# Gate and up products of the FFNs as groups of two by two tiles with seven products

## The reference

```python
def swiglu(u, w_gate, w_up, w_down):              # D_FF = 2816
    return (jax.nn.silu(u @ w_gate) * (u @ w_up)) @ w_down
for l in range(DEPTH):                            # DEPTH = 2
    mod = c_act @ w_ada[l] + b_ada[l]
    sh1, sc1, g1, sh2, sc2, g2, sh3, sc3, g3 = jnp.split(mod, N_MOD, axis=-1)
    x = x + 0.5 * g1 * swiglu(modulate(x, sh1, sc1), ffn1_gate[l], ffn1_up[l], ffn1_down[l])
    x = x + g2 * token_mix(modulate(x, sh2, sc2), ...)
    x = x + 0.5 * g3 * swiglu(modulate(x, sh3, sc3), ffn2_gate[l], ffn2_up[l], ffn2_down[l])
# hybrid layer, at its end: D_FF_2 = 4096
x = x + jnp.square(jax.nn.relu(h2 @ w_up)) @ w_down
```

## Time and profile before

| | |
|---|---|
| median of 3 runs | 3493.08 us (3489.26 to 3496.66) |
| profiled execution | 3486.15 us, of which the span is 3484.4 us |
| TensorE busy | 3432.2 us (99%) |
| VectorE busy | 1755.6 us (50%) |
| ScalarE busy | 1182.7 us (34%) |
| GpSimd busy | 269.2 us (8%) |
| clock granted to TensorE, mean | 0.992 |

### The profile page before, as it was taken

The page is one execution under the profiler, slowest core; times in us unless marked ns, Lnnn a source line. Parts: engine busy times, 40 slices in busy tenths (PEclk is TensorE's granted clock), DMA queues, the critical chain, the costliest instruction groups (busy, mean ns, idle before and its releaser), DMA issues.

```text
span 3484.4 us, 40863 instructions
## 1 busy us (share of the span) xinstructions
PE 3432.2 (99%) x16696; PEld 2744.1 (79%) x16696; DVE 1755.6 (50%) x3034; ACT 1182.7 (34%) x1989; POOL 269.2 (8%) x226
## 2 busy tenths in 40 slices
PE   8999999999999999999999999999999999999999
PEld 7888786777888788887777878887778777878887
DVE  7666456565666733334654643334553555364433
ACT  3222236543222222223555332223322444223322
POOL 0000210002000200021100100013011000120000
PEclk9999999999999999999999999999999999999999
DMA  7565321123565533233210322322221223122332
GB/s 251 206 209 187 105 92 60 43 68 120 189 218 194 184 99 101 93 95 105 74 49 25 115 85 85 109 83 93 73 85 64 72 65 120 40 94 91 98 102 79
DMA packets 120361, 376.36 MB, mean 108 GB/s; under 512 B 13296, under 2 KB 28272, under 8 KB 120176
## 3 DMA queue, kind: packets, MB, share of 16 engines
q1 hardware_dynamic: 120176, 373.76, 32.7%
HBM read 371.61 MB, written 2.10 MB: 107 GB/s over the span
## 4 chain that ended last, share of the span: by engine, by line
PE 93%; DVE 4%; ACT 2%; issue 0%; POOL 0%; DMA 0%; SPq 0%; ACTq 0%; POOLq 0%; DVEq 0%
PE ps L449 26%; PE ps L451 26%; PE ps L450 26%; PE ps L670 2%; PE ps L693 2%; PE ps L565 2%; PE ps L492 1%; PE ps L483 1%; PE ps L484 1%; PE ps L485 1%; PE ps L499 1%; DVE s_wl L1459 1%; PE ps L504 0%; ACT s_wh L961 0%; PE ps L532 0%
## 5 line engine op out<-in xcount | busy, mean ns | idle before, releaser
L1459 DVE TENSOR_TENSOR s_wl<-s_raw,s_wh 128x1024 fp32r<-128x1024 f32 (+3 forms) x645 | 704.8, 1094 | 892.7 <-ACT s_wh L961 891.9
L449 PE MATMUL ps<-s_uh,s_wh 128*128 128x512 f32 x2824 | 1129.8, 400 | 17.0 <-ACT s_sg L1201 4.5
L451 PE MATMUL ps<-s_ul,s_wh 128*128 128x512 f32 x2824 | 1106.3, 392 | 0.0
L450 PE MATMUL ps<-s_uh,s_wl 128*128 128x512 f32 x2824 | 1105.5, 391 | 0.0
L961 ACT ACTIVATE s_wh<-s_raw 128x1024 fp32r<-128x1024 f32 (+3 forms) x645 | 588.0, 913 | 734.5 <-PE ps L451 543.1
L449 PEld LDWEIGHTS ps<-s_uh,s_wh 128*128 128x128 f32 x2824 | 533.7, 189 | 161.0 <-issue 43.2
L451 PEld LDWEIGHTS ps<-s_ul,s_wh 128*128 128x128 f32 x2824 | 533.3, 189 | 113.4
L450 PEld LDWEIGHTS ps<-s_uh,s_wl 128*128 128x128 f32 x2824 | 533.9, 189 | 108.2 <-issue 2.2
L451 PE MATMUL ps<-s_fl,s_wh 128*128 128x512 f32 x960 | 378.2, 394 | 0.0
L449 PE MATMUL ps<-s_fh,s_wh 128*128 128x512 f32 x960 | 378.2, 394 | 0.0
L450 PE MATMUL ps<-s_fh,s_wl 128*128 128x512 f32 x960 | 378.2, 394 | 0.0
(11 more groups left out here) (406 smaller groups left out, 3342.6 us busy)
## 6 DMA issues: line engine op xcount, KB each, us to landing
s_raw<-w SPq DMA_DIRECT2D x616, 512.0 KB, 3.6
s_raw<-w SPq DMA_DIRECT2D x96, 192.0 KB, 2.4
s_raw<-w SPq DMA_DIRECT2D x64, 256.0 KB, 2.6
s_raw<-w SPq DMA_DIRECT2D x19, 128.0 KB, 2.1
s_x<-x SPq DMA_DIRECT2D x4, 512.0 KB, 6.8
out<-s_x SPq DMA_DIRECT2D x8, 256.0 KB, 2.5
s_raw<-w SPq DMA_DIRECT2D x4, 420.0 KB, 4.3
s_crow<-crow SPq DMA_DIRECT2D x2, 512.0 KB, 6.0
```

The lines of the kernel that those rows point to most:

```text
L449: TE.matmul(o, w_hi(i, k), h, start=first, stop=False)
L450: TE.matmul(o, w_lo(i, k), h, start=False, stop=False)
L451: return TE.matmul(o, w_hi(i, k), l, start=False, stop=last)
L1459: V.tensor_tensor(wl[w][:, 0:n], raw[t % NRAW][:, 0:n], wh[w][:, 0:n].bitcast(F32), SUB).then_inc(*s_lo.up(("lo", t)))
```

## The change

Two column tiles (A, B of the output), two tiles of input features (k1, k2) and two halves of the tokens (256 each) are a product of two 2x2 block matrices. Instead of eight block products it makes seven, between sums of weight blocks and sums of activation blocks (the Winograd form of Strassen's scheme), and combines the results. This holds for gate and up from column tile 2 on (from 6 on in `f10`, from 4 on in `up`); the tiles before are as they were, and so are the down products.

- A weight tile is now two feature tiles by 256 columns (128x512, 256 KB); there are four for a group of gate or up. VectorE and GpSimd extend it in place to seven blocks (128x896): VectorE one sum, GpSimd three differences. ScalarE and VectorE split 896 columns into high part and rest.
- The activation side has four block combinations for each pair of feature tiles (`th`, `tl`), made once a stage: GpSimd four differences of 128x256 for each of four pairs, from an unsplit copy `uu` that ScalarE now also writes; ScalarE the high part, VectorE the rest, beside the first plain column tiles.
- TensorE runs 21 matmuls of 256 columns a weight tile, into four banks for a group.
- Combining: ScalarE copies the first product out of PSUM, VectorE adds the others in four operations (`combine`). SiLU, product, high part and rest then handle 1024 columns at once.
- Rounds are 12 and 10 column tiles (12, 10, 10 in `up`).
- Side tiles: one behind every fourth weight tile of a group, one more behind the second tile of up where jj < 14, and as before behind plain and down tiles. `f20` keeps 48 of its 72, `f11` gets 24.

```diff
+SEVEN = ((0, 3, 0), (2, 0, 0), (5, 0, 1), (4, 1, 0), (1, 1, 1), (6, 2, 0), (3, 2, 1))
+def side_at(x, j, kp):
+    return kp == 3 or kp == 1 and x == "u" and j < 14
 # tensor_engine
+        def seven(g, name, c, banks, st):
+            o = [take((g, q), b) for q, b in enumerate(banks)]
+            for kp in range(4):
+                i = get(name, 2 * kp, c * 128)
+                pe.wait_ge(*s_dve["t", st, kp])
...
+                for n, ((unit, q, half), (h, l)) in enumerate(zip(SEVEN, right)):
+                    out = o[q][:, 256 * half:256 * half + 256]
+                    w = slice(128 * unit, 128 * unit + 128)
+                    TE.matmul(out, wh[slot[i]][:, w], h, start=kp == 0 and half == 0, stop=False)
+                    TE.matmul(out, wl[slot[i]][:, w], h, start=False, stop=False)
+                    ins = TE.matmul(out, wh[slot[i]][:, w], l, start=False, stop=kp == 3 and (half == 1 or q == 3))
 # scalar_engine, get
-                    act.wait_ge(*landed(t))
+                    act.wait_ge(*(s_pool["weights", t] if todo[t][5] == "seven" else landed(t)))
 # vector_engine, get
+            while added[0] <= min(i + NRAW - 1, len(todo) - 1):
+                t = added[0]
+                added[0] += 1
+                if todo[t][5] == "seven":
+                    w = raw[t % NRAW]
+                    dve.wait_ge(*landed(t))
+                    V.tensor_tensor(w[:, 512:640], w[:, 128:256], w[:, 384:512], ADD).then_inc(*s_dve.up(("S1", t)))
...
-                    n, w = todo[t][2] * todo[t][4], slot[t]
+                    n, w = 896 if todo[t][5] == "seven" else todo[t][2] * todo[t][4], slot[t]
+            def combine(x_, jj, q):
...
+                V.tensor_tensor(q[:, 0:5:4, :], q[:, 3:4, :].broadcast_to([128, 2, 256]), two_(0), ADD)...
+                dve.wait_ge(*s_pe["ps", (g_, "all")])
+                dve.wait_ge(*s_dve.now())
+                V.tensor_tensor(q[:, 1:3, :], q[:, 4:5, :].broadcast_to([128, 2, 256]), two_(1), ADD)...
+                dve.wait_ge(*s_dve.now())
+                V.tensor_tensor(q[:, 3, :], q[:, 2, :], bank((g_, 1))[:, 0:256], ADD)...
+                dve.wait_ge(*s_dve.now())
+                V.tensor_tensor(q[:, 1:3, :], q[:, 1:3, :], two_(2), ADD)...
 # pool_engine
+        def weights(st):
+            for kp in range(4):
...
+                PO.tensor_tensor(q[:, 0, :], k1[:, 256:512], k1[:, 0:256], SUB)...
+                PO.tensor_tensor(q[:, 1, :], k2[:, 256:512], q[:, 0, :], SUB)...
+                PO.tensor_tensor(q[:, 2, :], q[:, 1, :], k1[:, 0:256], SUB)...
+                PO.tensor_tensor(q[:, 3, :], k2[:, 0:256], q[:, 1, :], SUB)...
...
+                    pool.wait_ge(*s_dve["S1", i])
+                    PO.tensor_tensor(w(5), w(4), w(0), SUB).then_inc(*s_pool.up(("S2", i)))
+                    PO.tensor_tensor(w(1), w(0), w(1), SUB).then_inc(*s_pool.up(("S3", i)))
+                    pool.wait_ge(*s_pool["S2", i])
+                    PO.tensor_tensor(w(6), w(2), w(5), SUB).then_inc(*s_pool.up(("S4", i), ("weights", i)))
```

More of the change, by code:

```diff
@@ L7, with rounds, single, mixed_at @@
 AHEAD = 2
-CHUNK_FF = 11
+ROUND = 12
 def chunks(n, step):
     return [(a, min(step, n - a)) for a in range(0, n, step)]
+def rounds(nf):
+    return [(0, ROUND)] + [(a, min(10, nf - a)) for a in range(ROUND, nf, 10)]
+def single(u, first):
+    return 6 if first else 2 if u else 4
+def side_at(x, j, kp):
+    return kp == 3 or kp == 1 and x == "u" and j < 14
+def mixed_at(u, first):
+    if first:
+        return {4: ((0,), (1,)), 5: ((2,), (3,))}
+    return {0: ((0, 1), ()), 1: ((2,), (3,))} if u else {0: ((0, 1), ()), 2: ((2,), ()), 3: ((3,), ())}
+SEVEN = ((0, 3, 0), (2, 0, 0), (5, 0, 1), (4, 1, 0), (1, 1, 1), (6, 2, 0), (3, 2, 1))
 def plan():
@@ L30, in ffn @@
     def ffn(g, u, d, nf, ahead=False):
-        for a, n in chunks(nf, CHUNK_FF):
+        for a, n in rounds(nf):
             for j in range(a, a + n):
@@ L34, in ffn @@
                     continue
-                if j == 0 and u:
+                if j >= single(u, ahead):
+                    for x, name in (("g", g), ("u", u)) if u and j % 2 == 0 else (("g", g),) if j % 2 == 0 else ():
+                        for kp in range(4):
+                            t.append((name, 2 * kp, 2, j * 128, 256, "seven"))
+                            if side and side_at(x, j, kp):
+                                t.append(side.pop(0))
+                elif j == 0 and u:
                     pair(g, 0, u, 0)
@@ L518, in ffn @@
             tiles.side = list(ADA.get(st, []))
+            at = ring[1]
+            halves = [[ring[0][(at + 4 + q) % 8] for q in range(4)], [ring[0][(at + q) % 8] for q in range(4)]]
+            assert len(ring[0]) == 8
             if first:
@@ L536, in ffn @@
                             ins.then_inc(*s_pe.up(*([("w", i)] if n == 7 else []), *([("ps", f)] if k == 7 else [])))
-            for a0, n in chunks(nf, CHUNK_FF):
+            for a0, n in rounds(nf):
                 for jj in range(a0, a0 + n):
@@ L540, in ffn @@
                         continue
-                    if jj == 0:
+                    if jj >= single(u, first):
+                        if jj % 2 == 0:
+                            p = 0 if u else jj // 2 % 2
+                            seven(("g", st, jj), g, jj, halves[p], st)
+                            if u:
+                                seven(("u", st, jj), u, jj, halves[1], st)
+                            ring[1] = at + (4 if u or p else 0)
+                    elif jj == 0:
                         fm_pair(("g", st, 0), g, 0, ("u", st, 0) if u else ("g", st, 1), u or g, 0 if u else 1, ("u", st))
@@ L1571, in ffn @@
                     low(fl[:, j, :], s[:], fh[:, j, :], s_act["hh", st, jj], ("h", st, jj))
-                for m in range(8):
-                    fm(d, n, m, a0, st)
+                begin = max(a0, plain)
+                for jj in range(begin, a0 + n, 2):
+                    for kp in range(4):
+                        get(g, 2 * kp, jj * 128)
+                        if side_at("g", jj, kp):
+                            side(st)
+                        if jj > begin and kp == 0 and not u:
+                            product(jj - 2)
+                        if jj > begin and kp == (0 if u else 1):
+                            hidden(jj - 2, a0)
+                    combine("g", jj, quad[0 if u else jj // 2 % 2])
+                    for kp in range(4 if u else 0):
+                        get(u, 2 * kp, jj * 128)
+                        if side_at("u", jj, kp):
+                            side(st)
+                    if u:
+                        combine("u", jj, quad[1])
+                        product(jj)
+                last = a0 + n - 2
+                for m in range(8):
+                    for k0, nk in chunks(n, 8):
+                        get(d, a0 + k0, m * 128)
+                        side(st)
+                        if m == 0 and k0 == 0:
+                            if not u:
+                                product(last)
+                            hidden(last, a0)
                     gate = mod[:, MOD[st] + 16 + m:MOD[st] + 17 + m] if st in MOD else None
```

153 lines of the change are left out of this document (135 added, 18 removed).

## The result

The changed kernel takes 3702.4 us (median of 4 runs, 3695.4 to 3703.9) against 3491.2 us for the kernel before on the same chip: a ratio of 1.061, 95% interval 1.059 to 1.062, slower by 211 us. The profiled execution of the changed kernel is 3703.9 us, with a span of 3702.1, that is 218 us above the profiled one of before; its mean granted clock is 0.969 for 0.992.

The account below looks back on a forecast made before the run. TensorE bounds the kernel before; after the change VectorE was to set the pace. Pairs +107, round ends +17 and stage starts +15 us make +139 on 3493: 3632 us, range 3490 to 3710.

Parts of the forecast that it names:

- rival (D): Whole kernel: each turn costs 0.31 us and hits all VectorE operations, landing takes 3.6, TensorE's clock falls: 3758 us; chance 0.08.
- TensorE's gain: Gate and up: 21 matmuls of 256 columns at 119.7 ns make a pair 20.1 us for 21.75, 75 us less.
- Rival (C): Matmuls of 256 columns don't come under 129.6 ns, weight load setting the pace: 3647 us; inside the forecast's 0.70.
- VectorE sets these paces: Gate and up: VectorE's work, port losses and transfer wait set the time of a pair; +107 us over all pairs.
- The wait for a transfer: Inside up, VectorE's sum waits some 2.4 us for the buffer a side tile frees, once per three-side pair.
- The paces: Gate and up, us a pair: three side tiles 27.4, two 24.3, none 20.8, last FFN 24.1; +107 us in all.
- The turns: VectorE operations with two SBUF sources lose 0.27 us each to a pending GpSimd difference; 13 losses, 3.5 us a pair.
- The last FFN: Two groups there have two products and rests: 19.8 us plus 4.3 of port losses, 24.1 a pair for 21.75.
- The clock: TensorE's clock, 1.00 in the FFN windows before, falls in places only in the worse case that totals 3758 us.
- Starts and ends: FFN stages: late hidden values at round ends +17 us, activation sums and first weight sums at starts +15 us.
- (A): Gate and up: port turns cost nothing, GpSimd fitting into the combinings and waits: 3501 us; chance 0.10.
- (B): Side tile operations and buffer wait also stay hidden, TensorE sets the pace in all pairs: 3428 us; chance 0.12.

Follow-up runs that it names:

- both suspects small: Changed kernel with side tile operations over 128 columns and GpSimd's differences over 16, results incomplete: 3518.5 us, 1.009 of the kernel before.

## Why the prediction was right, and where its sizes were not

The forecast was 3632 us, in a range from 3490 to 3710; 3702 is inside, 8 us from its end, and on the side that had 0.80. The increase was 211 us where 139 were forecast. That it lies inside is partly luck: the pairs with side tiles (30.4 and 26.8 us) lie nearer to rival (D), 31.5 and 26.4, than to the forecast's 27.4 and 24.3, and two errors the other way, VectorE's work and the last FFN, kept the total down. Of the signs that the prediction named, VectorE is at 76% and not over 90% with side tiles, the lo pass has a mean of 1.20 and not 1.3 us, TensorE without side tiles is idle 8% and not 3%. By its steps:

- **TensorE's gain** was right: 119.7 ns from start to start for 256 columns was forecast, and the trace of the changed kernel has 26 steps in the 3.02 us between these two lines, 116.2 ns. So the pair is 19.5 to 19.7 us where TensorE bounds it (forecast 20.1). Rival (C), a floor of 129.6 ns, fell.

```profile
1639.95 0.28 PE L525 MATMUL ps<-s_uh,s_wh 128*128 128x256 f32 x1
...
1642.97 0.28 PE L527 MATMUL ps<-s_tl,s_wh 128*128 128x256 f32 x1
```

- **The step that failed** is "VectorE sets these paces": the pair was taken as VectorE's busy time plus one wait. Measured, a three-side pair has 23.0 us of VectorE's work, turns included (forecast 25.0), 2.3 us of waiting for a transfer (forecast 2.4), and 4.2 of waiting for ScalarE plus 0.9 of short gaps, which were in no term. So two errors of opposite sign: work and turns 2.0 us too much, the path VectorE, GpSimd, ScalarE, VectorE missing with 4 to 5. The prediction said itself that idle time of VectorE in side pairs would show it wrong, and it shows 24%. The wait for a transfer agrees in sum only: it was to be 2.4 us once a pair, and it is nine waits of 1.3 us in five pairs. (A small misreading beside it: the transfer at 905.63 is issued 0.03 us after the side operation's end, not 0.1.) The run with the sum one tile later shows that this path is real and what a tile of it is worth; the prediction had placed the sum "four ahead" and costed only its transfer, never asking how many tiles GpSimd and ScalarE have for their part.
- **The paces**: three sides 30.4 (27.4 forecast), two 26.8 with one three-side pair among the five and 26.6 without it (24.3), none 21.8 in `f11` and `f21` round 2 and 22.6 in `f21` round 1 (20.8), last FFN 21.8 (24.1). Sum of the pairs +170 for +107.
- **The turns** were right in kind and somewhat too dear: the lo pass of 896 columns has a mean of 1202 ns against 1.08 to 1.09 free, the sum 440 against 280, the product 1264. The free difference takes 0.45 to 0.47 us, not 0.40. Of the forecast, 13 turns at 0.27 us are 3.5 us a pair; with small differences VectorE's work in a pair without side tiles falls from 19.0 to 16.4, 2.7 us. "SBUF — State Buffer" of the Trainium skill (Who interferes with whom) calls the port pair that the two engines share an exclusive lock. The single cases here agree: the difference issued at 1005.37, with 0.92 us of the lo pass left, took 0.78 us longer than a free one. What was too dear is my estimate from it, 1.7 us a pair more than my turns: the sum over a pair comes to less than my turns, not more.
- **The last FFN** was the term mis-sized the other way: 24.1 forecast and 21.4 to 22.7 measured. In its window VectorE is busy 50.0 us in two and a half pairs, 20.0 each: its own 19.8 were right only with the turns in them, the 4.3 us on top were not there.
- **The clock.** The forecast left it at full speed in the likeliest case and had its fall in rival (D). It fell: 0.89 in the three-side round, 0.94 in the two-side one, and 1.00 where no side tiles are. TensorE stands 35.7 of 151.9 us there, and each of the eight falls in that round begins in or just behind a gap of 2.0 to 3.8 us; in the run with both suspects small the same round has 0.95. I could not separate what the clock costs, only bound it: the same 840 matmuls keep TensorE busy 116.2 us at 0.89 and 100.8 at 1.00, so by this it is some 3 us a pair at most; in the three-side rounds some 30 of a pair's 168 matmuls start 0.2 to 0.3 us after the one before, as at the lower level of 1.2 GHz, but part of that time TensorE would have waited anyway.
- **Starts and ends** were forecast at 17 + 15 = 32 us and measured 35.
- **Rivals (A) and (B)** fell: the turns cost, and the only rounds shorter than before are the last two of the last FFN, by 0.3 us a pair. With differences and side tiles made small (both) the kernel is still 0.9% slower than before: 983.0 us for the pairs, where before has 978.8, and the rest starts and ends.

What stays open: what bounds the three-side pair at 25.0 us with both made small, whether the depth of the raw ring (five) or the two tiles of lead of high part and lo pass. A deeper ring was not tried. No kernel of these beats the one before; the nearest with the whole computation is the one with seven products in `f21` and the last FFN only.

## What to carry to other kernels

When work is split over engines in a ring (VectorE's sum, GpSimd's differences, ScalarE's high part, VectorE's lo pass), costing the busiest engine is not enough: add up the path from the first to the last step, with the list positions of everything that stands between them, and compare it with the tiles of lead. Saved matmul time is worth nothing while the engines that make the operands have less slack than the operands' extra work: here 1.65 to 2.2 us a pair were to be had, and the sums, their turns and their path cost 2.2 to 10.8. Shifting the small sums between VectorE and GpSimd did not help in any of the three ways tried here: both stand on the same path.

## What was not expected of the hardware

A GpSimd difference of 16 columns still has a mean of 0.36 to 0.62 us in the two runs that made it small, against 0.65 to 0.95 for 128: an eighth of the columns leaves over half of the time, turns included.

And the clock can fall where the trace shows no gap of TensorE. In the last mixer, with code as before, TensorE of the changed kernel was busy all of 42 us, granted 0.67, for 186 matmuls; the same 186 took the kernel before 31.3 us at 0.94 (second row). The kernel with two sums on each engine, with the changed FFNs too, had 0.93 there and 31.4 us, so the change does not bring it every time; it put 11 us into one profiled execution:

```profile
3180.00:3222.00 42.00, 42.00 (x186) 34.53 (x187) 5.34 (x6) 5.55 (x8) 4.64 (x5) 0.67 0.04 13
```
```profile
2983.70:3015.00 31.30, 31.30 (x186) 26.20 (x187) 4.70 (x6) 5.56 (x8) 5.69 (x5) 0.94 0.05 17
```

In the same mixer two more of the thirteen profiles with the change have 17 us in a row at the lower level of the clock (1.2 GHz) (four sums on GpSimd, and seven products in `f21` and the last FFN alone).
